# Sparse attention and its filler projections: how many steps run beside each head

## The chip, the cores and the metric

The kernel runs on one core of a Trainium2 chip. The metric is the device time of one execution in microseconds (us). Three executions of the kernel before gave 1282.54, 1283.15 and 1283.22 us; the median is 1283.15 us.

## The reference, cut to what matters

A first block (sequence of 256 tokens, width 1024) projects the normed input once and splits the result. Eight sparse-attention heads in two groups use three branches, a retention branch uses four heads, and two sets of merge gates weigh the branches:

```python
proj = h @ w_in
q_nsa, kv_nsa, g_nsa, q_ret, k_ret, v_ret, g_ret, g_merge = split(proj)
# compressed branch: 15 blocks of keys; softmax over them, per head
p_cmp = masked_softmax(q @ kc.T * scale, mask_cmp);  o_cmp = p_cmp @ vc
# selected and window branches: both see all causal keys at this length
o_slc = masked_softmax(q @ k_slc.T * scale, causal) @ v_slc
o_win = masked_softmax(q @ k_win.T * scale, causal) @ v_win
o = g0 * o_cmp + g1 * o_slc + g2 * o_win
```

The projections that fill TensorE's time beside the heads are `v_ret` (two units of 512 columns, `vr0` and `vr1`), `g_ret` (`sg0`, `sg1`) and the first quarter of `g_merge` (`gm0`, `gm1`, 256 columns each). Retention, a feed-forward block, and then two layers of another network follow; the change doesn't touch them.

## The kernel before

**Weights.** All weights are packed in chunks of at most 128x2048 f32 and come over SP's queue into six `raw` buffers. ScalarE (ACT) rounds a chunk to `whi` (L1102), VectorE (DVE) or GpSimd subtracts to get the rest, `wlo` (L1761 on DVE), and TensorE multiplies three times for each product: high by high, high by low, low by high. In the stage of the change all splits are DVE's. Each engine's program runs strictly in its written order. A split is written `AHEAD` = 3 chunks before the use: whoever takes chunk i in the back queue first splits all up to i + 3. ACT's `whi` must also wait until the chunk four back has been used up.

**The back queue.** `rows` (L545) yields after each two products of three matmuls with 512 columns: a unit of two chunks is eight steps, four for each chunk. `feats` (L566) yields after one k: six matmuls with 256 columns, eight steps for a unit of one chunk. The queue beside the heads is `vr0` (steps 1 to 8), `vr1` (9 to 16), `sg0` (17 to 24), `sg1` (25 to 32), `gm0` (33 to 40) and `gm1` (41 to 48). The first step of each chunk (1, 5, 9, ..., 29, 33, 41) splits the chunk three on; on DVE step 5 splits none and step 9 splits two. A finished half of a unit is copied out of PSUM, the first half by DVE (steps 6, 14, 22, 30), the second half by ACT (8, 16, 24, 32); a finished gate unit by ACT (40, 48).

**The front.** PE, ACT and DVE each have a generator `nsa` (L792, L1299, L2092) that emits its own part of the attention, and `weave` (L205) runs a number of back steps at each yield: two if nothing else is said. There are two blocks of 128 tokens. For each, `compressed` makes the scores of the compressed branch (PE), their softmax (DVE and ACT), the transpose of the probabilities (L747) and the product with the values. Then come eleven places s for the eight heads u: at place s, PE transposes the probabilities of head s-2 (L776), multiplies those of head s-3 with the values, and makes the scores of head s (both L528). DVE at place s copies the transposed probabilities of head s-2 out if s is even (`ET`, L1803), gathers four heads' outputs if s-3 is the fourth (L2075 to L2089, `Tm` first), and takes the maximum of head s (L2059). ACT at place s copies `ET` of head s-2 if s is odd (L1296) and takes the exponentials of head s (L1288). Places run from 0 to 10 for the first block and from 8 to 18 for the second.

**What waits for what.** The transpose of head u waits for its exponentials and for `ET` of head u-1 (one bank holds them). The values of head u wait for `ET` of head u and, for u = 4 or 12, for `Tm` of the head before. The scores of head u wait for the exponentials of head u-2.

With two steps at each yield, PE's queue of 48 steps ends after place 13. Places 14 to 18 have none beside them.

The two loops that decide it:

```python
def weave(front, back, n):
    for m in front:
        steps(back, n if m is None else m)
    run(back)
```

Of the kernel before, what the change touches and what calls it, by code (L numbers as in the profile page):

```python
# [132 lines left out]
class Count:  # L133
# [6 lines left out]
    def at(self, sem, *names, by=1):  # L140

        self.now[sem] += by
        self.name(sem, *names)
        return SEM.get(sem), by
# [7 lines left out]
    def on(self, *name):  # L152

        return ("d_out", 0) if self.known is None else self.known[name]
# [35 lines left out]
def run(g):  # L190
    for _ in g:
        pass
# [7 lines left out]
def steps(g, n):  # L200
    for _ in range(n):
        next(g, None)

def weave(front, back, n):  # L205

    for m in front:
        steps(back, n if m is None else m)
    run(back)

def bc(ap, shape, ax):
# [7 lines left out]
def tok(tt):  # L220
    return slice(tt * 128, tt * 128 + 128)
# [284 lines left out]
def pe_program(pe, t, ev, pb):  # L506
# [20 lines left out]
    def product(o, a, b, start=True, stop=True, names=()):  # L527
        signalled(pe.op.matmul(o, a, b, start=start, stop=stop, skip_group_check=True), names, "pe_small")  # L528
# [148 lines left out]
    def ret_turned(w, tt):  # L677
        turned((w, "T", tt), [(w, "rot", tt)], t.ra[2 * (w == "kr") + tt][:, :], 4)
# [55 lines left out]
    def compressed(tt):  # L734
        for k in range(2):
            pe.wait_ge(*on("free", ("qT", k, 1)))
            pe.wait_ge(*on("free", ("kT", k)))
        pe.wait_ge(*on("kc lo"))
        if tt:
            pe.wait_ge(*on("exp", 6))  # L740
        for j in range(8):
            product(t.sc[0][:, j * 32:j * 32 + 32], t.q1[:, j, tok(tt)], t.kcs[:, :, j % 2, :],
                    names=[("cmp scores", tt)] * (j == 7))
        yield
        pe.wait_ge(*on("cp", tt))
        pe.wait_ge(*on("VC") if tt == 0 else on("ET", 7))
        pe.op.transpose(t.tp[0:120, 0:128], t.cp[:, :], ident).then_inc(*at("pe_turned", ("cpT", tt)))  # L747
        yield
        pe.wait_ge(*on("cpT out", tt))
        if tt:  # L750
            pe.wait_ge(*on("Tm", 7))
        product(t.ob[:, :], t.cpT[:, :], t.VC[:, :, :], names=[("o cmp", tt)])
        yield

    def scores(u):
        tt, hd = units[u]
        gr, b, n = hd // 4, hd % 4, 128 * (tt + 1)
        bk = t.sc[u % 2]
        for k in range(2):
            pe.wait_ge(*on("free", ("kT", k)))  # L760
        pe.wait_ge(*on("cmp masked", tt) if u % 8 < 2 else on("exp", u - 2))
        for k in t.k1h, t.k1l:
            product(bk[:, :].rearrange("p (a k) -> p a k", a=2)[:, :, 0:n], t.q1[:, 2 * b + gr, tok(tt)],
                    k[:, gr, :, 0:n], k is t.k1h, False)
        pe.wait_ge(*on("idb"))
        pe.wait_ge(*on("mkb"))
        for a in range(2):
            product(bk[:, a * S + n - 128:a * S + n], t.idb[:, :], t.mkb[:, :], False, True, [("scores", u)] * a)

    def probs_turned(u):  # L770
        nk = units[u][0] + 1
        pe.wait_ge(*on("exp", u))
        pe.wait_ge(*on("cpT out", units[u][0]) if u % 8 == 0 else on("ET", u - 1))
        for a in range(2):
            for k in range(nk):
                ins = pe.op.transpose(t.tp[:, (a * nk + k) * 128:(a * nk + k) * 128 + 128],  # L776
                                      t.Ex[u % 3][:, a, k * 128:k * 128 + 128], ident)
        ins.then_inc(*at("pe_turned", ("ExT", u)))

    def values(u):  # L780
        tt, hd = units[u]
        gr, nk = hd // 4, tt + 1
        pe.wait_ge(*on("ET", u))
        if u % 4 == 0:
            pe.wait_ge(*on("oa cmp", tt) if u % 8 == 0 else on("Tm", u - 1))
        for a in range(2):
            for k in range(nk):
                product(t.ob[:, ((hd % 4) * 2 + a) * 64:((hd % 4) * 2 + a) * 64 + 64], t.ET[u % 2][:, a * nk + k, :],
                        t.qkv[k][:, 896 + 256 * a + 64 * gr:896 + 256 * a + 64 * gr + 64], k == 0, k == nk - 1,
                        [("pv", u)] * (a == 1 and k == nk - 1))  # L790

    def nsa():  # L792
        yield
        n = 0
        for tt in range(2):
            for _ in compressed(tt):
                yield
                n += 1
                if n == 3:
                    ret_turned("kr", 0)  # L800
            for s in range(8 * tt, 8 * tt + 11):
                if 8 * tt <= s - 2 < 8 * tt + 8:
                    probs_turned(s - 2)
                if 8 * tt <= s - 3:
                    values(s - 3)
                if s < 8 * tt + 8:
                    scores(s)
                yield
                n += 1
                if n == 5:  # L810
                    ret_turned("kr", 1)
# [264 lines left out]
def act_program(act, t, ev, pb):  # L1076
# [222 lines left out]
    def nsa():  # L1299
        yield  # L1300
        n = 0
        for tt in range(2):
            for _ in compressed(tt):
                yield
                n += 1
                if n == 3:
                    ret_turned("kr", 0)
            for s in range(8 * tt, 8 * tt + 11):
                if 8 * tt <= s - 2 < 8 * tt + 8 and s % 2:
                    probs_out(s - 2)  # L1310
                if s < 8 * tt + 8:
                    exps(s)
                yield
                n += 1
                if n == 5:
                    ret_turned("kr", 1)
# [411 lines left out]
def dve_program(dve, t, ev, pb):  # L1728
# [288 lines left out]
    def compressed(tt):  # L2017
        madd, m01 = (small(t, n).rearrange("p (t c) -> p t c", t=2)[:, tt, 0:15] for n in ("madd", "m01"))
        mx, l, r = t.rt[:, 0:8], st[:, 480:488], st[:, 488:496]
        dve.wait_ge(*on("cmp scores", tt))  # L2020
        s = t.sc[0][:, 0:256].rearrange("p (b g a c) -> p g b a c", g=2, a=2, c=16)[:, :, :, :, 0:15]
        cs4 = t.cs[:, :, :].rearrange("p (g b) c -> p g b c", g=2)
        dve.op.tensor_tensor(cs4, s[:, :, :, 0, :], madd.unsqueeze(1).unsqueeze(1).to_broadcast([128, 2, 4, 15]),
                             ALU.add).then_inc(*at("dve_small"))
        await_own()
        dve.op.tensor_tensor(cs4, s[:, :, :, 1, :], cs4, ALU.add).then_inc(*at("dve_small", ("cmp masked", tt)))
        await_own()
        dve.op.tensor_reduce(mx, t.cs[:, :, :], AXX, ALU.max).then_inc(*at("dve_small"))
        await_own()
        dve.op.tensor_tensor(t.cs[:, :, :], t.cs[:, :, :], bc(mx, [128, 8, 15], 2), ALU.subtract).then_inc(  # L2030
            *at("dve_small", ("cs less max", tt)))
        yield None if tt else 0
        dve.wait_ge(*on("cs exp", tt))
        dve.op.tensor_reduce(l, t.cs[:, :, :], AXX, ALU.add).then_inc(*at("dve_small"))
        await_own()
        dve.op.reciprocal(r, l).then_inc(*at("dve_small"))
        await_own()
        dve.wait_ge(*on("gates"))
        dve.op.tensor_tensor(r, r, gates[:, tt, :, 0], ALU.mult).then_inc(*at("dve_small"))
        if tt:  # L2040
            dve.wait_ge(*on("cpT", 0))
        dve.op.tensor_tensor(t.cp[:, :].rearrange("p (h c) -> p h c", h=8), t.cs[:, :, :], bc(m01, [128, 8, 15], 1),
                             ALU.mult).then_inc(*at("dve_small", ("cp", tt)))
        if tt == 0:
            yield 4
        copied([("cpT out", tt)], t.cpT[0:120, :], t.tp[0:120, 0:128], ("cpT", tt))
        yield
        yield
        dve.wait_ge(*on("o cmp", tt))
        await_own()  # L2050
        dve.op.tensor_tensor(t.oa[tt][:, :].rearrange("p (h d) -> p h d", h=8),
                             t.ob[:, :].rearrange("p (h d) -> p h d", h=8), bc(r, [128, 8, 64], 2),
                             ALU.mult).then_inc(*at("dve_out", ("oa cmp", tt)))
# [38 lines left out]
    def nsa():  # L2092
        yield 0
        for tt in range(2):
            yield from compressed(tt)
            for s in range(8 * tt, 8 * tt + 11):
                if 8 * tt <= s - 2 < 8 * tt + 8 and s % 2 == 0:
                    probs_out(s - 2)
                if 8 * tt <= s - 3 and (s - 3) % 4 == 3:
                    values(s - 3)  # L2100
                if s < 8 * tt + 8:
                    score_max(s)
                yield

    qr_read, kr_read = ([(w, "T", tt) for tt in range(2)] for w in ("qr", "kr"))
    back = chain(
# [541 lines left out]
```

## Time and profile before

| | before |
|---|---|
| runs (3) | 1282.54, 1283.15, 1283.22 us; median 1283.15 us |
| profiled execution, its own time | 1283.58 us |
| its span, first to last instruction | 1282.3 us |
| mean granted TensorE clock | 0.999 |
| PE busy | 1270.8 us (99% of the span) |
| DVE busy | 891.4 us (70%) |
| ACT busy | 689.4 us (54%) |
| PE's share of the chain that ended last | 95% |

The profiled execution took 0.4 us more than the median; 1.3 us of its time lie outside the span. A row of the timeline gives start, duration, engine, line, operation, output and inputs, shapes, and in brackets the idle time before it and what ended that. The stage of the change lies between about 84 and 170 us. All times of rows are us from the start of the span. Ends of matmuls are modelled, so the distance between two starts tells more of PE than the durations do.

### The profile page before, as it was taken

How to read it: one execution, taken by the hardware profiler on the slowest of the kernel's cores; microseconds unless marked ns; L12 is line 12 of the kernel's file. 1: busy time of each engine (PE TensorE's matmuls, PEld its weight loads, DVE VectorE, ACT ScalarE, POOL GpSimd, SP SyncE).
4: the chain of work that ended last, by engine and by line, in shares of the span. 5: the costliest groups of instructions: out<-in, count | busy, mean ns of one | idle time of the engine just before them, and what ended most of it. 6: DMA issues, size and time to landing. Idle time of an engine off the chain costs nothing.

```text
span 1282.3 us, 20063 instructions
## 1 busy us (share of the span) xinstructions
PE 1270.8 (99%) x8232; PEld 1152.3 (90%) x8232; DVE 891.4 (70%) x1308; ACT 689.4 (54%) x992; POOL 357.6 (28%) x270
## 2 busy tenths in 40 slices
PE   8999999999999999999999999999999999999999
PEld 7988889989999879899998888888999999888887
DVE  6765665768888468986567777646898476877752
ACT  6655445366655355466746555435456674655541
POOL 0210021014440059476450000007857633000000
PEclk9999999999999999999999999999999999999999
DMA  9654234555555546734464555544854444555551
GB/s 348 235 191 152 110 116 142 187 185 193 177 186 196 192 143 235 235 134 155 141 213 165 197 181 183 194 164 175 280 184 139 158 154 176 189 177 192 196 190 42
DMA packets 36572, 230.83 MB, mean 180 GB/s; under 512 B 4480, under 2 KB 5120, under 8 KB 10496
## 3 DMA queue, kind: packets, MB, share of 16 engines
q1 hardware_dynamic: 36480, 229.55, 50.6%
q8 instruction: 65, 1.06, 0.3%
q14 instruction: 27, 0.22, 0.0%
HBM read 222.19 MB, written 1.05 MB: 174 GB/s over the span
## 4 chain that ended last, share of the span: by engine, by line
PE 95%; DVE 2%; DMA 1%; POOL 1%; ACT 1%; SPq 0%; issue 0%; DVEq 0%; POOLq 0%
PE ps L604 13%; PE ps L582 12%; PE ps L584 12%; PE ps L583 12%; PE ps L523 11%; PE ps L525 11%; PE ps L524 11%; PE ps L607 7%; PE ps L528 5%; PE ps L542 1%; DMA raw<-in_w 1%; PE ps L1014 1%; SPq L428 0%; PE ps L776 0%; POOL sg L1658 0%
## 5 line engine op out<-in xcount | busy, mean ns | idle before, releaser
L1102 ACT ACTIVATE whi<-raw 128x2048 fp32r<-128x2048 f32 x205 | 390.2, 1906 | 164.8 <-PE ps L525 95.7
L1761 DVE TENSOR_TENSOR wlo<-raw,whi 128x2048 fp32r<-128x2048 f32 (+1 forms) x165 | 379.8, 2304 | 135.8 <-ACT whi L1102 134.9
L582 PE MATMUL ps<-hh,whi 128*128 128x256 f32 x992 | 283.6, 286 | 0.0
L584 PE MATMUL ps<-hh,wlo 128*128 128x256 f32 x992 | 280.7, 283 | 0.0
L583 PE MATMUL ps<-hh,whi 128*128 128x256 f32 x992 | 280.6, 283 | 0.0
L1636 POOL TENSOR_TENSOR wlo<-raw,whi 128x512 fp32r<-128x512 f32 x160 | 203.6, 1304 | 135.6 <-ACT whi L1102 132.6
L604 PE MATMUL ps<-hh,whi 128*128 128x512 f32 x704 | 192.6, 395 | 0.0
L583 PEld LDWEIGHTS ps<-hh,whi 128*128 128x128 f32 x992 | 190.1, 192 | 0.4 <-issue 0.2
L582 PEld LDWEIGHTS ps<-hh,whi 128*128 128x128 f32 x992 | 190.1, 192 | 0.4 <-issue 0.2
L584 PEld LDWEIGHTS ps<-hh,wlo 128*128 128x128 f32 x992 | 190.1, 192 | 0.0
L1608 POOL TENSOR_TENSOR st<-st,sm 128x1 f32<-128x1 f32 (+2 forms) x28 | 48.3, 1725 | 403.2 <-DVE st L1814 310.7
L604 PEld LDWEIGHTS ps<-hh,whi 128*128 128x128 f32 x704 | 120.4, 189 | 16.3
L607 PEld LDWEIGHTS ps<-hh,wlo 128*128 128x128 f32 x704 | 108.0, 189 | 15.0
L523 PE MATMUL ps<-whi,hh 128*128 128x512 f32 (+1 forms) x272 | 108.8, 400 | 3.3 <-DVE hh L1873 1.4
L607 PE MATMUL ps<-hh,wlo 128*128 128x256 f32 x704 | 112.0, 281 | 0.0
L525 PE MATMUL ps<-whi,hh 128*128 128x512 f32 (+1 forms) x272 | 105.2, 387 | 0.0
L524 PE MATMUL ps<-wlo,hh 128*128 128x512 f32 (+1 forms) x272 | 105.2, 387 | 0.0
L523 PE MATMUL ps<-whi,ghi 128*128 128x512 f32 x264 | 102.9, 390 | 0.0
L524 PE MATMUL ps<-wlo,ghi 128*128 128x512 f32 x264 | 102.7, 389 | 0.0
L525 PE MATMUL ps<-whi,glo 128*128 128x512 f32 x264 | 102.7, 389 | 0.0
L2362 DVE SCALAR_TENSOR_TENSOR ps<-gp,sm,ps 128x256 f32<-128x256 f32 x232 | 99.3, 483 | 0.0
L1424 ACT ACTIVATE fu<-ps 128x512 f32<-128x512 f32 x44 | 26.3, 598 | 108.4 <-PE ps L607 108.4
(311 smaller groups left out, 2099.3 us busy)
## 6 DMA issues: line engine op xcount, KB each, us to landing
raw<-in_w SPq DMA_DIRECT2D x203, 1024.0 KB, 4.8
raw<-in_w SPq DMA_DIRECT2D x8, 256.0 KB, 6.3
kst<-kh SPq DMA_DIRECT2D x16, 128.0 KB, 2.6
qst<-qh SPq DMA_DIRECT2D x16, 128.0 KB, 2.4
raw<-in_w SPq DMA_DIRECT2D x2, 560.0 KB, 16.8
x<-in_x SPq DMA_DIRECT2D x2, 512.0 KB, 5.1
gain<-in_rows SPq DMA_DIRECT2D x2, 512.0 KB, 10.7
kst<-kl SPq DMA_DIRECT2D x8, 128.0 KB, 2.5
```

Of the source, the lines that this page charges most:

```text
L523: pe.op.matmul(o, sh, mh, start=start, stop=False, skip_group_check=True)
L524: pe.op.matmul(o, sh, ml, start=False, stop=False, skip_group_check=True)
L525: signalled(pe.op.matmul(o, sl, mh, start=False, stop=stop, skip_group_check=True), names)
L582: pe.op.matmul(o, wh[:, k, c:c + 128], hi[:, k, :], start=first, stop=False, skip_group_check=True)
L583: pe.op.matmul(o, wh[:, k, c:c + 128], lo[:, k, :], start=False, stop=False, skip_group_check=True)
L584: ins = pe.op.matmul(o, wl[:, k, c:c + 128], hi[:, k, :], start=False, stop=last, skip_group_check=True)
L604: pe.op.matmul(o[:, :], wh[:, k, c], t.hh[:, k, :, :], start=k == 0, stop=False, skip_group_check=True)
L607: ins = pe.op.matmul(o[:, 0:S], wl[:, k, c], t.hhi[:, k, :], start=False, stop=k == 7, skip_group_check=True)
L1102: act.op.activation(t.whi[i % NHI][:, 0:n], t.raw[i % NRAW][:, 0:n], ACT.Copy).then_inc(*at("act_hi", ("hi", i)))
L1636: pool.op.tensor_tensor(t.wlo[i % NRAW][:, half(k)], t.raw[i % NRAW][:, half(k)], t.whi[i % NHI][:, half(k)].bitcast(F32), ALU.subtract).t ...
L1761: dve.op.tensor_tensor(t.wlo[i % NRAW][:, c], t.raw[i % NRAW][:, c], t.whi[i % NHI][:, c].bitcast(F32), ALU.subtract).then_inc(*at("dve_lo ...
L2362: ins = dve.op.scalar_tensor_tensor(t.cv[:, f, :] if j == 30 else acc, t.gp[:, f, j:j + S], cw[:, f, j:j + 1], acc, ALU.mult, ALU.add)
```

## The change

A new function gives the number of steps beside a place, and the three `nsa` generators yield it after each place. PE's `compressed` yields 2 + tt after the scores, and PE's `nsa` hands on what it yields; ACT's and DVE's `compressed` are as before.

```diff
+def beside(s):
+    return 1 if 3 <= s < 8 else 2

@@ PE, compressed(tt), after the compressed scores
-        yield
+        yield 2 + tt
         pe.wait_ge(*on("cp", tt))
@@ PE, nsa()
-            for _ in compressed(tt):
-                yield
+            for m in compressed(tt):
+                yield m
@@ PE, ACT and DVE, nsa(), after each place s
-                yield
+                yield beside(s)
```

Steps done when a place (or a yield of `compressed`) is over, as the two programs write them:

| | s=2 | 3 | 4 | 5 | 6 | 7 | 8 | 9 | 10 | compressed: 1, 2, 3 | 8 | 9 | 10 | 11 | 12 | 13 | 14 | 15 |
|---|---|---|---|---|---|---|---|---|---|---|---|---|---|---|---|---|---|---|
| before, all three engines | 14 | 16 | 18 | 20 | 22 | 24 | 26 | 28 | 30 | 32, 34, 36 | 38 | 40 | 42 | 44 | 46 | 48 | | |
| after, PE | 14 | 15 | 16 | 17 | 18 | 19 | 21 | 23 | 25 | 28, 30, 32 | 34 | 36 | 38 | 40 | 42 | 44 | 46 | 48 |
| after, ACT and DVE | 14 | 15 | 16 | 17 | 18 | 19 | 21 | 23 | 25 | 27, 29, 31 | 33 | 35 | 37 | 39 | 41 | 43 | 45 | 47 |

## Rows read from the trace of the kernel before

**Rows 1.** The page, part 1: busy time of each engine.
```profile
PE 1270.8 (99%) x8232; PEld 1152.3 (90%) x8232; DVE 891.4 (70%) x1308; ACT 689.4 (54%) x992; POOL 357.6 (28%) x270
```

**Rows 2.** Waits of PE in the whole run, first row: total us, times, longest.
```profile
PE ps L523 <- DVE hh L1873: 1.4, 1, 1.4
```

**Rows 3.** Timeline of PE, place 3 of the first block and place 4's start.
```profile
105.52 0.38 PE L776 MATMUL ps<-sm,Ex 128*128 128x128 f32 x2
...
106.11 0.37 PE L528 MATMUL ps<-k1h,q 128*128 128x256 f32 x1
...
106.53 0.48 PE L523 MATMUL ps<-whi,hh 128*128 128x512 f32 x1
...
109.35 0.38 PE L776 MATMUL ps<-sm,Ex 128*128 128x128 f32 x2
```

**Rows 4.** Timeline of DVE, places 4 to 6 of the first block.
```profile
110.58 0.42 DVE L2059 TENSOR_REDUCE st<-ps 128x2 f32<-128x256 f32 x1 [0.39 <-PE ps L528]
113.75 2.29 DVE L1761 TENSOR_TENSOR wlo<-raw,whi 128x2048 fp32r<-128x2048 f32 x1 [2.75 <-ACT whi L1102]
115.96 0.42 DVE L2059 TENSOR_REDUCE st<-ps 128x2 f32<-128x256 f32 x1
117.45 0.42 DVE L1803 COPY ET<-ps 128x256 f32<-128x256 f32 x1 [1.07 <-PE ps L776]
...
118.22 0.69 DVE L2081 TENSOR_TENSOR Tm<-ps,st 128x512 f32<-128x512 f32 x1
...
119.75 0.42 DVE L2059 TENSOR_REDUCE st<-ps 128x2 f32<-128x256 f32 x1
```

**Rows 5.** Timeline of ACT, place 4 of the first block, later a copy and a `whi`.
```profile
111.04 0.37 ACT L1288 ACTIVATE Ex<-ps,st 128x128 f32<-128x128 f32 x1 [0.39 <-DVE st L2059]
...
111.74 1.91 ACT L1102 ACTIVATE whi<-raw 128x2048 fp32r<-128x2048 f32 x1
...
126.87 0.60 ACT L1135 ACTIVATE sg<-ps 128x512 f32<-128x512 f32 x1
...
131.81 1.92 ACT L1102 ACTIVATE whi<-raw 128x2048 fp32r<-128x2048 f32 x1 [2.27 <-PE ps L525]
```

**Rows 6.** Timeline of PE, from the first block's last values to place 16.
```profile
131.55 0.55 PE L528 MATMUL ps<-qkv,ET 128*128 128x64 f32 x4
...
139.20 0.32 PE L747 MATMUL ps<-sm,cp 128*120 128x128 f32 x1 [0.61 <-DVE cp L2042]
...
143.08 0.40 PE L528 MATMUL ps<-k1h,q 128*128 128x512 f32 x1
...
145.15 0.40 PE L528 MATMUL ps<-k1h,q 128*128 128x512 f32 x1
...
147.23 0.60 PE L776 MATMUL ps<-sm,Ex 128*128 128x128 f32 x4
...
149.75 0.60 PE L776 MATMUL ps<-sm,Ex 128*128 128x128 f32 x4
...
165.57 0.63 PE L776 MATMUL ps<-sm,Ex 128*128 128x128 f32 x4 [1.40 <-ACT ET L1296]
```

**Rows 7.** Timeline of DVE, from the end of the first block to place 9.
```profile
133.83 2.29 DVE L1761 TENSOR_TENSOR wlo<-raw,whi 128x2048 fp32r<-128x2048 f32 x1
...
136.64 0.27 DVE L2023 TENSOR_TENSOR cs<-ps,sm 128x120 f32<-128x120 f32 x1
...
145.95 0.69 DVE L2059 TENSOR_REDUCE st<-ps 128x2 f32<-128x512 f32 x1 [1.34 <-PE ps L528]
```

**Rows 8.** Timeline of ACT, place 10 of the second block.
```profile
149.19 0.47 ACT L1288 ACTIVATE Ex<-ps,st 128x256 f32<-128x256 f32 x1 [1.00 <-DVE st L2059]
...
150.10 1.91 ACT L1102 ACTIVATE whi<-raw 128x2048 fp32r<-128x2048 f32 x1
```

**Rows 9.** Stretches: busy us of PE, PEld, DVE, ACT, POOL; granted clock; DMA share; GB/s.
```profile
10.00:11.00 1.00, 1.00 (x3) 0.72 (x3) 1.00 (x6) 1.00 (x3) 0.00 (x0) 0.50 1.03 260
...
160.00:169.90 9.90, 8.47 (x69) 7.49 (x68) 5.07 (x12) 5.52 (x14) 0.00 (x0) 1.00 0.32 108
```

More of the change, by code:

```diff
@@ L1312, in nsa @@
                     exps(s)
-                yield
+                yield beside(s)
                 n += 1
@@ L2102, in nsa @@
                     score_max(s)
-                yield
+                yield beside(s)
     qr_read, kr_read = ([(w, "T", tt) for tt in range(2)] for w in ("qr", "kr"))
```

## The prediction

> **What bounds the kernel.** I read the page first: PE is busy 99% of the span, DVE 70%, ACT 54% [rows 1]. The change adds and removes no work, so it can only change how long PE waits. The list of PE's waits says how little that is: its first row is a single wait of 1.4 us [rows 2]. The timelines show those in the stage of the change: 0.61 us ahead of the transpose of the second compressed softmax and 1.40 us ahead of place 16's transpose, which is among the places with no steps beside them [rows 6]. Even if both went, the gain is 2.0 us. About 0.2%, 2.6 us, is what a measurement of this kernel can tell from no change. So the question is whether the thinner places 3 to 7 and the shifted weight splits make new waits.
>
> **Prices.** A place of the first block takes 109.35 - 105.52 = 3.83 us: 1.01 us until its first projection matmul and 2.82 us for two row steps, 1.40 each. The scores start 0.59 us into the place [rows 3]. A place with one step takes 2.43. From the scores on, the way through the other engines is: maximum 0.64 us after the scores' start (109.35 + 0.59 = 109.94 to 110.58) [rows 3, 4], exponentials 0.46 later, and 0.70 for them until ACT takes its next instruction [rows 4, 5]. A `whi` on ACT is followed by its `wlo` on DVE 2.01 us after its own start, and DVE's next instruction starts 2.21 after that of the `wlo` [rows 4, 5]. A split that a place emits thus blocks ACT and DVE for 4.2 us in all, and every maximum and `ET` copy behind it in the program waits. Before, the split of step 17 stood at place 4, between the maxima of heads 4 and 5, and nothing was late: head 5's transpose was due at 105.52 + 4 x 3.83 = 120.84, and its `ET` 4 was copied from 117.45 [rows 4].
>
> **Part 1, places 3 to 7.** Up to place 3 nothing differs. Places 4, 5, 6 and 7 then start at 107.95, 110.38, 112.81 and 115.24. Step 17 is now place 5's, behind the maximum and the exponentials of head 5 and ahead of `ET` 4, the gathering of heads 0 to 3 and the maximum of head 6. Scores 5 start at 110.97, maximum 111.61, exponentials 112.07, `whi` 112.77, `wlo` 114.78, `ET` 4 116.99. With 0.42 us for the copy and 0.1 for the signal, the transpose of head 5, due at 115.24, starts at 117.5: a wait of 2.3 us. The values of head 4 come 0.22 us later but need `Tm` 3, which starts 0.77 us after `ET` 4 and lasts 0.69 [rows 4]: to 118.45, a second wait of 0.7. From `ET` 4 to maximum 6 it is 2.3 us (119.75 - 117.45, the gathering of four heads between them) [rows 4], so the exponentials of head 6 are at 119.8 and `ET` 5 stands behind them on ACT; the transpose of head 6 is due at 120.7 and gets its bank at 121.0: 0.25. Together **+3.25 us**. From below 0, if that `wlo` came 3.3 us sooner; from above 3.6, since nothing else is queued there. I take 3.25: each link is a row of the same stage.
>
> **Part 2, the compressed softmax.** In the kernel before, the last values of the block start at 131.55, the `wlo` of step 29 follows the gathering at +2.28, the softmax starts at +5.09 and the transpose at +7.65 [rows 6, 7]. After, place 10 runs steps 24 and 25: the split is step 25's, and its `whi` needs the chunk that step 24 uses up, in the same place, 0.4 (four value matmuls, most of the 0.59 of [rows 3]) + 1.40 after the values' start. Before, the chunk was used up when the values started, and the `whi` followed 0.26 later (131.81) [rows 5, 6]; so 0.26 for the signal, and 0.5 for ACT's copy of `sg0`, which now stands ahead (0.60 long [rows 5]; the next instruction starts about 0.1 before such an end): `whi` at +2.56, `wlo` +4.57. DVE's own copy of `sg1` (0.6) is no longer ahead of the softmax. So the softmax starts at +4.57 + 2.21 = +6.78 and the transpose at 6.78 + (139.20 - 136.64) = +9.34, 1.69 later than before. PE arrives one row step, 1.40, later. The wait thus grows: **+0.3 us**, although PE has three steps there. Bounds: -0.6 (the whole wait goes, if the copy and the split are hidden) and +0.8.
>
> **Part 3, places 8 to 11 of the second block.** Take U for the start of that transpose (before: 139.20). Before, places up to the scores of head 8 took 143.08 - 139.20 = 3.88 with four gate steps at 0.72; after, four row steps: 3.88 + 4 x (1.40 - 0.72) = 6.6. Then places 8, 9 and 10 are 2.07, 2.08 and 2.52 us long [rows 6], with gate steps as before: the transpose of head 9 is due at U + 6.6 + 6.67 = U + 13.27. But step 33, whose split stood well ahead of the heads, is now emitted at place 8, behind maximum 8 and the exponentials of head 8, with ACT's copy of `sg1` also before it. Maximum 8 at U + 6.6 + 0.80 [rows 6, 7] = 7.4; exponentials 0.72 later, 0.91 long [rows 8]: 9.03; the copy 0.5: 9.53; `wlo` +2.01: 11.54; maximum 9 +2.21: 13.75; exponentials 14.47, and 0.9 for them: 15.4. Head 9's transpose waits from 13.27 to 15.45: **+2.2 us**. `ET` 8 is ready at 15.1, just before. Bounds: 0 (if `whi` went ahead of the exponentials, which its place in the program excludes) and 2.5.
>
> **Part 4, the tail.** Step 41's split is at place 12 and 4.2 us long in the same way; but there a full place is about 3.4 us long (2.52 [rows 6] and eight value matmuls), and before it stood at place 10 without a wait. I find the transpose of head 13 due 0.1 us after its exponentials. Places 14 and 15 now have two gate steps each, 1.45 us a place, so the 1.40 us ahead of place 16 are covered but for some 0.3 us in the gathering of four heads; what follows place 16 is as before. **-1.4 us**, between -1.7 and -0.8.
>
> **POOL and SP.** Nothing of POOL's or SP's is moved: raw loads are issued when chunks are used up, six ahead, and no split in this stage waited for one.
>
> **Sum.** 3.25 + 0.3 + 2.2 - 1.4 = +4.35 us. On the profiled execution's 1283.58 that gives 1287.9; the median of the runs is 0.4 lower, so I say **1287.5 us**, 0.34% slower.
>
> **Rival 1: the clock falls as well.** Near the start of the run PE stood idle for 1.4 us, and right after it the granted clock was 0.50, that is 1.2 instead of 2.4 GHz [rows 2, 9]. With the 1.40 us wait in the tail it stayed at 1.00 [rows 9]. The waits of parts 1 and 3 are 2.2 to 3 us of idleness in a stretch of about 3. If it then stays low for three microseconds (assumed; the row shows one), 1.5 us of PE's work are lost: with one of the two +5.9, with both +7.3: 1289 or 1290.5. The rows hold one case of each kind, with the shorter idleness. The Trainium skill ("TensorE: Matmul & The Clock Gate", The HAM clock gate) says that the throttled state is the default and activity releases it; by that rule a long enough hole costs more than itself, which speaks for this rival.
>
> **Rival 2: only one of the two new waits comes.** If ACT or DVE catch up 2 us somewhere, for instance since a split starts sooner than the rows let me place it, the sum is +2.1 (part 1 alone) or +1.1 (part 3 alone): 1284.2 to 1285.3, within 0.2%.
>
> **Rival 3: not slower.** The places decide: if the `wlo` of step 17 began by 112.5 instead of 114.8 and that of step 33 by U + 9.3 instead of U + 11.5, neither transpose would wait, and part 4 alone would count, with part 2: -1.1, 1282.0 us. For it speaks that ACT is busy for only 54% of the run [rows 1]; against it, that the idle time is before instructions which wait for DVE and PE in turn, and the split stands behind these. The Trainium skill ("TensorE: Matmul & The Clock Gate", the table at its head) says ScalarE's and VectorE's queues are strictly first in, first out; that is what the rows show, where maximum 5 starts the moment `wlo` lets DVE go (115.96, 2.21 after the `wlo`) [rows 4] though its scores were made 1.5 us sooner. A gain of more than 0.2% needs every wait of the stage to go, and there are only 2.0 us of them.
>
> **How the numbers follow.** Forecast (both waits, clock kept) 0.50; rival 1 0.20; rival 2 0.15, two thirds of it within 0.2%; rival 3 0.11; something faster that I don't see 0.04. Slower by over 0.2%: 0.50 + 0.20 + 0.05 = 0.75, less 0.02 for the low end of my own forecast. The likeliest case alone is 1286.3 to 1288.5. The range goes down into rival 2 and up through rival 1: 1284.0 to 1290.5.
>
> **What would show it.** After: no wait of 1.4 us for `ET` on ACT at place 16; in its place a wait of about 2.3 us of PE L776 for DVE's `ET` (L1803) and one of L528 for `Tm` in the first block near 117 us; about 2.2 us of L776 for ACT's exponentials (L1288) some 13 us behind the compressed transpose; that transpose's own wait at 0.6 to 1.1. Place 16's transpose (165.57 before) should be at about 169.9, and every later stage as long as before. It would be wrong if `wlo` of step 17 is not between maximum 5 and `ET` 4 on DVE, if the transposes of heads 5 and 9 start without a wait, or if later stages change length.

## The result, and the profile after

| | before | after |
|---|---|---|
| median | 1283.15 us | 1288.38 us |
| runs (5 each) | 1282.54 to 1283.53 | 1286.56 to 1289.38 |
| profiled execution, its own time | 1283.58 us | 1289.06 us |
| its span | 1282.3 us | 1287.8 us |

The medians are 5.23 us apart, 0.41%; the ratio on record, which isn't the quotient of the medians, is 1.0036, with an interval of 1.0023 to 1.0049, or 4.6 us. All rows below give times from the start of the span. The lines of after are six higher than before's (L776 is L782, L528 is L534, L1803 is L1809, L1761 is L1767, L2059 is L2065, L2081 is L2087, L1288 is L1294).

The page's engine totals of after say that the work is the same as before [rows 1]:

```profile
PE 1271.3 (99%) x8232; PEld 1152.4 (89%) x8232; DVE 891.1 (69%) x1308; ACT 689.5 (54%) x992; POOL 357.7 (28%) x270
```

PE's waits in the whole run, after (engine, line, what it waited for: total us, times, longest). Before, the longest was 1.4 us [rows 2]; now two of 2.1 head the list, and the 1.4 us for `ET` on ACT is gone:

```profile
PE ps L782 <- ACT Ex L1294: 2.1, 1, 2.1
PE ps L782 <- DVE ET L1809: 2.1, 1, 2.1
...
PE ps L753 <- DVE cp L2048: 0.9, 1, 0.9
...
PE ps L534 <- DVE Tm L2087: 0.5, 1, 0.5
```

The timeline of PE, after, from place 3 of the first block to place 16 of the second:

```profile
105.08 0.38 PE L782 MATMUL ps<-sm,Ex 128*128 128x128 f32 x2
...
117.20 0.41 PE L782 MATMUL ps<-sm,Ex 128*128 128x128 f32 x2 [2.05 <-DVE ET L1809]
...
118.14 1.01 PE L534 MATMUL ps<-qkv,ET 128*128 128x64 f32 x4 [0.53 <-DVE Tm L2087]
...
122.09 0.38 PE L782 MATMUL ps<-sm,Ex 128*128 128x128 f32 x2
...
128.96 0.55 PE L534 MATMUL ps<-qkv,ET 128*128 128x64 f32 x4
...
138.26 0.33 PE L753 MATMUL ps<-sm,cp 128*120 128x128 f32 x1 [0.91 <-DVE cp L2048]
...
153.73 0.66 PE L782 MATMUL ps<-sm,Ex 128*128 128x128 f32 x4 [2.11 <-ACT Ex L1294]
...
171.21 0.63 PE L782 MATMUL ps<-sm,Ex 128*128 128x128 f32 x4
```

These are the transposes of head 5 (117.20), head 6 (122.09), the second compressed softmax (138.26), head 9 (153.73) and place 16 (171.21), the last now with nothing in brackets. What DVE does ahead of the first wait, after:

```profile
111.26 0.42 DVE L2065 TENSOR_REDUCE st<-ps 128x2 f32<-128x256 f32 x1 [1.71 <-PE ps L534]
114.43 2.29 DVE L1767 TENSOR_TENSOR wlo<-raw,whi 128x2048 fp32r<-128x2048 f32 x1 [2.75 <-ACT whi L1108]
116.64 0.42 DVE L1809 COPY ET<-ps 128x256 f32<-128x256 f32 x1
...
117.40 0.69 DVE L2087 TENSOR_TENSOR Tm<-ps,st 128x512 f32<-128x512 f32 x1
```

Maximum of head 5, then `wlo`, then `ET` 4. Before, the `wlo` stood between the maxima of heads 4 and 5, with as long an idle time before it, and cost nothing [rows 4]. Two things differ: what is queued behind it, and that PE comes back for the `ET` sooner, since the places are thin. Both are needed, by an estimate from the prediction's own prices [rows 3, 4, 5]: with full places and the split behind maximum 5, `ET` 4 would be copied at about 119.8 and ready some 0.5 us before head 5's transpose is due (120.84), and only `Tm` would be about 0.2 late. No run tried that. Stretches of the two holes, after (us, busy us of PE, PEld, DVE, ACT, POOL, granted clock, DMA share, GB/s):

```profile
116.00:119.00 3.00, 1.27 (x7) 1.06 (x7) 2.86 (x8) 0.00 (x0) 0.00 (x0) 0.88 0.00 0
119.00:122.00 3.00, 3.00 (x11) 2.47 (x11) 0.77 (x3) 1.85 (x9) 0.00 (x0) 0.55 0.00 0
122.00:126.00 4.00, 4.00 (x25) 3.34 (x23) 0.42 (x1) 1.60 (x1) 0.00 (x0) 1.00 0.15 25
151.00:154.00 3.00, 0.89 (x8) 0.69 (x7) 2.82 (x4) 1.17 (x5) 0.00 (x0) 1.00 0.00 0
154.00:157.00 3.00, 3.00 (x27) 2.73 (x26) 0.69 (x1) 1.72 (x6) 0.00 (x0) 1.00 0.02 5
```

Behind the first hole the granted clock is 0.55, which is nearly all 1.2 GHz; behind the second, where PE did even less, it stays at 1.00. So this execution shows the forecast and, once, the clock of rival 1. (In stretches of 1 us the clock is below 1.00 from 118 to 122 and nowhere else in this run; the profiled execution of before has its only such stretches at 9 to 14, near the start of the run.)

**The stage's length** is a measure that leaves the rest of the run out: from place 3's transpose to the first scores of the retention that follows the second block. Before it is 63.81 us (105.52 to 169.33), after 69.88 (105.08 to 174.96): 6.07 longer, while the span is 5.5 longer and the stage begins 0.44 sooner.

### The profile page after: what moved, and what is told of

Its sections match the earlier page's. It is cut to its first block, busy times and chain, and to the rows that moved or that the text cites. A ratio compares the mean times of both kernels' runs of the same rounds, so it can differ in the third digit from the quotient of the medians.

```text
span 1287.8 us, 20063 instructions
## 1 busy us (share of the span) xinstructions
PE 1271.3 (99%) x8232; PEld 1152.4 (89%) x8232; DVE 891.1 (69%) x1308; ACT 689.5 (54%) x992; POOL 357.7 (28%) x270
## 4 chain that ended last, share of the span: by engine, by line
PE 95%; DVE 2%; ACT 2%; DMA 1%; POOL 1%; issue 0%; SPq 0%; DVEq 0%; POOLq 0%
PE ps L610 13%; PE ps L588 12%; PE ps L590 12%; PE ps L589 12%; PE ps L529 11%; PE ps L531 11%; PE ps L530 11%; PE ps L613 6%; PE ps L534 5%; PE ps L548 2%; PE ps L1020 1%; DVE wlo L1767 1%; DMA raw<-in_w 0%; ACT whi L1108 0%; PE ps L782 0%; POOL sg L1664 0%
## 5 line engine op out<-in xcount | busy, mean ns | idle before, releaser
L1767 DVE TENSOR_TENSOR wlo<-raw,whi 128x2048 fp32r<-128x2048 f32 (+1 forms) x165 | 379.6, 2304 | 140.0 <-ACT whi L1108 139.3
```

The lines of the kernel that those rows point to most:

```text
L1767: dve.op.tensor_tensor(t.wlo[i % NRAW][:, c], t.raw[i % NRAW][:, c], t.whi[i % NHI][:, c].bitcast(F32), ALU.subtract).then_inc(*at("dve_lo ...
```

## The experiments

The theory (T): each new wait is made by DVE's `wlo`, which stands in the program ahead of an `ET` or a maximum that PE will soon need, and holds DVE until ACT's `whi` is done. The ten kernels e1 to e10 are described one by one below. Rivals: the order of PE against the other engines makes the waits (P); the granted clock makes most of the time (C); thinner places are harmful by themselves, since each leaves less of PE's work above a head's way through the other engines (B). Ratios are to the kernel before on the same chip, as they are on record; they aren't the quotients of the medians, and differ from them by up to 0.0008 (e5). Before took 1283.3, 1283.8 and 1282.6 us in the three batches (29, 26 and 23 runs).

| kernel | median us (runs) | ratio, interval | stage us |
|---|---|---|---|
| e1 | 1291.16 (6) | 1.0057, 1.0039 to 1.0074 | 71.74 |
| e2 | 1281.88 (12) | 0.9987, 0.9974 to 1.0000 | 64.66 |
| e3 | 1280.34 (12) | 0.9976, 0.9966 to 0.9986 | 61.39 |
| e4 | 1283.59 (12) | 1.0002, 0.9990 to 1.0015 | 64.67 |
| e5 | 1285.55 (12) | 1.0006, 0.9994 to 1.0019 | 65.24 |
| e6 | 1287.64 (12) | 1.0029, 1.0018 to 1.0039 | 67.55 |
| e7 | 1289.05 (9) | 1.0035, 1.0023 to 1.0048 | 71.49 |
| e8 | 1297.61 (6) | 1.0102, 1.0087 to 1.0117 | 77.63 |
| e9 | 1288.84 (12) | 1.0046, 1.0030 to 1.0063 | 69.60 |
| e10 | 1287.27 (12) | 1.0029, 1.0018 to 1.0039 | 68.40 |

One caution for all of them. The kernel before itself takes 1282 to 1288 us on these chips, and its time goes with its mean granted clock: in the three batches the executions at 0.998 or more have medians of 1282.4, 1282.9 and 1282.5 us, those at 0.997 or less 1286.0, 1286.5 and 1287.5. Medians of kernels that drew different shares of the two can't be set beside each other to within 2 us. The waits of the profiled executions can. The stage's length can once the clock's part in it is told, for it is of one execution only, and not always a typical one: e5's and e6's were the fastest of their twelve (1283.85 and 1285.44 us) and held the clock longer than most, e2's (1284.70) was among the slowest. And not all of this scatter is of the stage: in the profiled executions of before, e1, e3, e4 and e8 the clock also fell between 9 and 18 us, where all kernels are alike, in e3 for about 7 us and only there.

### One part of the change at a time: e1, e2

e1 leaves out the extra steps of PE's compressed softmax:

```diff
@@ PE, compressed(tt)
-        yield 2 + tt
+        yield 2
```

> The changed kernel with PE's compressed branch back at two steps; the thin places 3 to 7 stay, so PE, ACT and DVE now do the same number of steps everywhere. Theory (new waits come from where the weight splits of steps 17, 25 and 33 stand among the heads): the waits for ET 4 and Tm 3 near head 5 stay as in the changed kernel (about 2.1 and 0.5 us); PE reaches the compressed transpose one row step (1.4 us) sooner while DVE's chain is as late, so that wait grows from 0.9 to about 2.5 us; the wait of head 9's transpose shrinks by 0.7 to about 1.5 us, since one more row step is done before it; a gate step more is left for the tail. In all 0 to +0.7 us against the changed kernel, 1288 to 1289. Rival (PE running one step ahead of ACT and DVE is what makes the waits): head 9's wait goes and the time falls to about 1286.

e2 keeps those and makes every place full again:

```diff
 def beside(s):
-    return 1 if 3 <= s < 8 else 2
+    return 2
```

> The kernel before with only PE's extra step after the second compressed scores; two steps at every place. Theory: no split moves, so no new wait; the 0.6 us ahead of the compressed transpose is covered by the gate step (0.7), place 13 has one step less and its successors come sooner, the 1.4 us wait at place 16 stays. 1282.2 to 1283.1, -0.7 to 0 us. Rival (PE ahead of ACT and DVE costs): over +1 us, with a wait of a transpose for exponentials near head 9.

Timeline of PE, e1, the compressed transpose and head 9's:

```profile
140.43 0.32 PE L753 MATMUL ps<-sm,cp 128*120 128x128 f32 x1 [2.27 <-DVE cp L2048]
...
155.89 0.66 PE L782 MATMUL ps<-sm,Ex 128*128 128x128 f32 x4 [1.43 <-ACT Ex L1294]
```

The wait for `cp` is 1.36 longer than in after, one row step. That prices the extra step: PE's third step covers 1.4 us of the softmax, and the thinner places are what made the softmax late. Head 5's transpose waits 2.1 us with or without that step (118.11), so the order of PE (P) makes none of the first hole. Nor does it make the second: head 9's wait is 1.43 without that step, where P wanted it gone. e1's time is 2 us above its expectation, and its stage 1.86 longer than after's. Some 1.3 of this is behind head 5, where the stretches show the clock low for two whole stretches, not one, and 0.6 is the gate step left for the tail (place 16's transpose to the end of the stage: 4.36 us against 3.75).

```profile
119.00:122.00 3.00, 2.95 (x11) 2.66 (x12) 1.61 (x4) 1.65 (x8) 0.00 (x0) 0.50 0.00 0
```

The next, 122 to 125, is at 0.50 too. In e2 the compressed wait is gone and the one in the tail stays. In its profile the clock fell behind that 1.40 us wait, which it had not in before's. The row is from e2's timeline of PE:

```profile
164.14 0.63 PE L782 MATMUL ps<-sm,Ex 128*128 128x128 f32 x4 [1.40 <-ACT ET L1302]
```

and this from e2's stretches:

```profile
166.00:169.00 3.00, 3.00 (x17) 3.00 (x16) 0.00 (x0) 2.40 (x2) 0.00 (x0) 0.51 0.04 8
```

The stage is 64.66 long for that reason: 63.81 less the 0.61 of the compressed wait, and 1.5 of clock. e2's ratio is 0.13% below 1, with 1 at the edge of its interval; its median is 0.3 us below what was expected.

### The places kept, the low parts moved: e3 and e4

e3 is the changed kernel, e4 the kernel before, each with one edit on DVE: a split asked for in a back step is emitted three steps later. (While `held_back` holds a list, `splits` only notes down what it was asked for.)

```diff
@@ DVE
+    held_back = [None]
+
     def splits(last):
 
+        if held_back[0] is not None:
+            held_back[0].append(last)
+            return
...
+    def later(g, n, only):
+        due, step = [], 0
+        while True:
+            step += 1
+            held_back[0] = []
+            over = next(g, "over") == "over"
+            asked, held_back[0] = held_back[0], None
+            for last in asked:
+                due.append((step + (n if not only or step in only else 0), last))
+            while due and (due[0][0] <= step or over):
+                splits(due.pop(0)[1])
...
-    weave(nsa(), back, 2)
+    weave(nsa(), later(back, 3, ()), 2)
```

> The changed kernel, but DVE emits each low-part split of this queue three steps later than ACT emits its whi; no step of PE or ACT moves. Theory (the split blocks DVE between a maximum and the ET copy while ACT's whi is still running): wlo of step 17 then stands at place 8, that of step 33 at place 10, both with their whi long done. The waits before heads 5 and 9 go, that before the compressed transpose goes (chain at +7.1 against PE's arrival at +8.2 after the last values), and only some 0.2 us of the tail wait is left: 1281 to 1282, -1 to -2 us against before and -7 against the changed kernel. Rival (a place with one step is too short for the chain scores, maximum, exponentials, ET whatever is split where): the waits before heads 5 to 7 stay, over 1286.

> The kernel before with the same lateness of DVE's low-part splits (three steps). Theory: before, the full places hide the splits anyway, so lateness alone gains nothing: the compressed chain keeps one wlo inside it (0.6 us wait stays), the 1.4 us of place 16 come from the gathering of four heads and stay. 1282.7 to 1283.5, within 0.5 us of before. Rival (late low parts are a gain by themselves, so that the third run's result says nothing about the moved steps): 1 us or more below before.

Timeline of DVE, e3 (its lines are five higher again: L1814 is `ET`, L2070 the maximum, L1772 `wlo`):

```profile
114.29 0.42 DVE L1814 COPY ET<-ps 128x256 f32<-128x256 f32 x1 [1.18 <-PE ps L782]
...
119.24 0.42 DVE L1814 COPY ET<-ps 128x256 f32<-128x256 f32 x1 [1.22 <-PE ps L782]
119.58 2.28 DVE L1772 TENSOR_TENSOR wlo<-raw,whi 128x2048 fp32r<-128x2048 f32 x1
```

`ET` 4 is copied at 114.29 instead of 116.64, though this stage began 1.38 us later (106.46), DVE waits for PE and no longer the other way, and the `wlo` has no idle time before it: `whi` was long done. PE's waits in the whole run of e3 hold no L782 and no L753:

```profile
PE ps L529 <- DVE hh L1884: 2.0, 1, 2.0
PE ps L548 <- DVE xn L1833: 1.2, 1, 1.2
PE ps L649 <- POOL zero L1626: 1.0, 1, 1.0
PE ps L534 <- DVE STt L2168: 0.8, 1, 0.8
```

The stage is 61.39 us, 8.5 less than after's and 2.4 less than before's. At 1280.34 us e3 beats both kernels, 0.24% below before and 0.7 us below the expected range. Of the 3.0 us by medians some 0.8 go with the clock: 10 of e3's 12 executions are at 0.998 or more, 20 of before's 29, and among those alone it is 1280.26 against 1282.45, 2.2 us, near the stage's 2.4. Places 3 to 7 are as thin in e3 as in the changed kernel, so B falls in their case: the thinning costs nothing once no `wlo` that must wait for its `whi` stands in the way. And e4 shows that lateness alone brings nothing: with the steps where they were, the tail's wait of 1.40 stays and the compressed one grows from 0.61 to 1.48, more than expected. Waits of PE, e4:

```profile
PE ps L747 <- DVE cp L2047: 1.5, 1, 1.5
PE ps L776 <- ACT ET L1296: 1.4, 1, 1.4
```

### One split at a time: e5 and e6

Both are the changed kernel with the same wrapper, in e5 for step 17's split alone, in e6 for step 33's:

```diff
-    weave(nsa(), back, 2)
+    weave(nsa(), later(back, 3, (17,)), 2)
```

> The changed kernel with DVE's wlo of step 17 alone emitted three steps later (at place 8 instead of place 5). Theory: the waits for ET 4 and Tm 3 go, with what follows them (3.25 us and, where the clock fell there, about 1.5 more); the compressed wait (0.9), head 9's (2.1) stay. 1283.7 to 1285.3. Rival (thin places are too short by themselves): the wait before head 5 stays, 1288.

> The changed kernel with DVE's wlo of step 33 alone emitted three steps later (place 10 instead of place 8). Theory: head 9's wait of 2.1 us goes, all else stays: 1286.0 to 1286.6, 2.1 us below the changed kernel. Rival (head 9 waits because its place comes too soon after the scores, not for the split): no change, or a wait of the same length for the exponentials.

First row of PE's waits in e5, and then in e6, where each took away one of after's two:

```profile
PE ps L782 <- ACT Ex L1294: 2.1, 1, 2.1
```

```profile
PE ps L782 <- DVE ET L1814: 2.1, 1, 2.1
```

In e5 the wait for `Tm` went too, and the clock stayed up: the stage fell by 4.64 (2.05 + 0.53, the clock's 1.5 and 0.5 more). In e6, where the clock fell behind the first hole as in after, it fell by 2.33, against a wait of 2.11. So each hole belongs to one split, as T says. By its ratio e5 is 0.06% above before (by the medians 0.14%), and its 1285.55 us are a little over what I expected. In e6 the median fell only from 1288.38 to 1287.64 where 2.1 us were expected; 11 of its 12 executions had a mean clock of 0.997 or less, and by the time alone e6 is inconclusive.

### Is it the split, or the places? e8 and e9

If T holds, other thin places must make a hole elsewhere: where the split of step 21 then falls.

```diff
-    return 1 if 3 <= s < 8 else 2
+    return 1 if 5 <= s < 10 else 2
```

> The changed kernel with the thin places at 5 to 9 instead of 3 to 7. Theory (the wait follows the split): step 17's split is back at place 4 and hurts nobody; step 21's now stands at place 7, ahead of ET 6, so heads 5 and 6 pass without a wait and the transpose of head 7 waits about 2.8 us for ET 6 on DVE; the compressed wait and head 9's stay. 1287 to 1288.5. Rival (it is head 5, with the gathering of heads 0 to 3 behind it, that can't stand a thin place): places 5 and 6 are still thin, so the wait stays at heads 5 and 6.

This edit reaches further than it should have: places 8 and 9 of the second block are thin as well, which no theory's numbers had counted. The whole time (1297.61 us, where 1287 to 1288.5 were expected; three waits of `ET`, the longest 3.5) thus tests nothing, though the first block already has its one wait at head 7 (125.34, 2.65). e9 limits it to the first block, with `1 if tt == 0 and 5 <= s < 10 else 2`:

> As the run with thin places 5 to 9, but in the first block only; that run thinned places 8 and 9 of the second block as well, which I had overlooked, and three waits for ET came of it. Steps from place 10 on are now those of the changed kernel. Theory (the wait follows the split): no wait before heads 5 and 6, 2.7 us before head 7's transpose for ET 6 (as that run's trace showed), 0.9 before the compressed transpose, 2.1 before head 9's. The sum of the waits is that of the changed kernel less 0.2, so 1286.5 to 1289. Rival (thin places late in the block are worse in themselves): 1291 or more, with further waits.

Timeline of DVE and then of PE, e9:

```profile
112.67 2.29 DVE L1767 TENSOR_TENSOR wlo<-raw,whi 128x2048 fp32r<-128x2048 f32 x1 [2.75 <-ACT whi L1108]
114.87 0.42 DVE L2065 TENSOR_REDUCE st<-ps 128x2 f32<-128x256 f32 x1
...
118.28 0.42 DVE L2065 TENSOR_REDUCE st<-ps 128x2 f32<-128x256 f32 x1 [0.37 <-PE ps L534]
121.63 2.29 DVE L1767 TENSOR_TENSOR wlo<-raw,whi 128x2048 fp32r<-128x2048 f32 x1 [2.92 <-ACT whi L1108]
123.84 0.42 DVE L1809 COPY ET<-ps 128x256 f32<-128x256 f32 x1
```

```profile
112.10 0.38 PE L782 MATMUL ps<-sm,Ex 128*128 128x128 f32 x2
...
114.58 0.38 PE L782 MATMUL ps<-sm,Ex 128*128 128x128 f32 x2
...
117.05 0.38 PE L782 MATMUL ps<-sm,Ex 128*128 128x128 f32 x2
...
119.53 0.38 PE L782 MATMUL ps<-sm,Ex 128*128 128x128 f32 x2
...
124.40 0.41 PE L782 MATMUL ps<-sm,Ex 128*128 128x128 f32 x2 [2.65 <-DVE ET L1809]
```

The transposes of heads 3 to 6 start 2.47 us apart with nothing in brackets, and that of head 7 waits 2.65: the hole moved by two places with the split behind maximum 7. Before it stand three thin places in a row without a wait. The three rows "maximum, `wlo`, `ET`" are in the same order as in after. And the `wlo` of step 17 (112.67), back ahead of maximum 5, costs nothing although thin places follow. Its 1288.84 us are within the expected range.

### The clock: e7 and e10

e7 adds, ahead of head 5's transpose, 16 matmuls on operands that are ready, into a bank whose contents are not used; they change no result and keep PE at work during the hole. e10 adds as many ahead of head 9's.

```diff
@@ PE, nsa()
             for s in range(8 * tt, 8 * tt + 11):
+                if s in (7, 11):
+                    pe.wait_ge(*(on("exp", 5) if s == 7 else on("oa cmp", 1)))
+                    for _ in range(16):
+                        product((t.sc[1] if s == 7 else t.ob)[:, 0:256], t.q1[:, 0, tok(0)], t.k1h[:, 0, 0, :])
```

(e7 has `if s == 7` and the first of each pair.)

> The changed kernel with 16 matmuls of 256 columns (some 1.9 us) added on PE ahead of head 5's transpose, where it waits 2.05 us; they write a bank that the scores of head 7 then overwrite, and change no result. Theory (the granted clock fell after that hole, and matmuls at 0.43 instead of 0.23 us cost 1.3 to 1.5 us): the transpose starts as late as before, the clock stays at 1.00 between 116 and 122 us, and the time falls by about 1.3 us to 1286.5 to 1287.3, with less scatter. Rival (the clock's fall is hidden by the next wait, and the scatter has another cause): 1288 to 1289 as the changed kernel.

> The changed kernel with the 16 filler matmuls ahead of head 5's transpose and 16 more ahead of head 9's, into a bank that head 8's values then overwrite. Theory (each hole can let the granted clock fall, and one filled hole left the fall to the other): the clock is 1.00 through the whole stage, every mean clock is 0.998 or above, the transposes start as late as before, and the median is 1286.3 to 1287.5, below both the changed kernel (1288.4) and the run with one filled hole (1289.1). Rival (the scatter has other causes than the holes): median still 1288 to 1289 with mean clocks of 0.997 and below.

Stretches of e7. Behind the first hole, now filled, the clock is 1.00; behind the second, where after's profile had 1.00, it fell:

```profile
119.00:122.00 3.00, 3.00 (x18) 2.36 (x18) 1.12 (x4) 1.78 (x9) 0.00 (x0) 1.00 0.00 0
150.00:153.00 3.00, 0.89 (x6) 0.74 (x5) 2.35 (x4) 1.64 (x7) 0.00 (x0) 0.86 0.00 0
153.00:156.00 3.00, 3.00 (x15) 2.48 (x13) 0.00 (x0) 1.00 (x3) 0.00 (x0) 0.50 0.00 0
```

The stage is 71.49 us long, 1.6 more than after's, since the clock was low for some 7 us here. So the time of e7 is no better than after's, and my expectation of a gain was a miss: the hole of head 9 can take the clock down too. It needn't, for in e5's profile, where it is the only hole as here, the clock stayed up. In e10 both are filled. Its stretches:

```profile
116.00:119.00 3.00, 2.35 (x17) 1.82 (x16) 2.86 (x9) 0.12 (x1) 0.00 (x0) 1.00 0.00 0
119.00:122.00 3.00, 3.00 (x18) 2.31 (x17) 0.61 (x2) 1.65 (x9) 0.00 (x0) 1.00 0.00 0
...
150.00:153.00 3.00, 2.81 (x26) 2.61 (x24) 1.83 (x4) 2.15 (x9) 0.00 (x0) 1.00 0.00 0
```

The median is as expected; 10 of its 12 executions have a mean clock of 0.998 or more, where all were expected to. The matmuls fill the holes but leave the cause, so what remains over before is the late transposes alone: 4.6 us by the stage (68.40 - 63.81), and 4.6 by the medians of the executions at 0.998 or more (1287.16 against 1282.53). C is thus the smaller part: 1.5 us between the two profiled stages (69.88 - 68.40). By the ratios (1.0036 of after, 1.0029 of e10) it would be 0.9 us of the whole, but their intervals overlap, and the whole times don't show it.

## Why the prediction came out right

It said 1287.5 us, and the median is 1288.38, within the range; the sum was +4.35, and +5.2 came by the medians, +4.6 by the ratio. In e10, where the clock holds, the stage is 4.59 longer than before's: that is what the sum was worked out for. Step by step:

- **Part 1** (+3.25). The `wlo` of step 17 is between maximum 5 and `ET` 4. Head 5's transpose starts 12.12 us after place 3's, where 11.98 was worked out; the waits are 2.05 and 0.53, where 2.3 and 0.7 stood. The third wait, 0.25 at head 6, isn't there: the low clock behind the hole made PE later than its bank. In e7, with the clock up, head 6's transpose comes 2.46 us after the values before it, where a thin place has 2.26, so some 0.2 of it is. The whole part is 3.16 there: 15.53 us from place 3's transpose to head 6's, against 12.37 in e5. e5 shows that the split of step 17 makes both waits.
- **Part 2** (+0.3). From the last values to the compressed transpose 9.30 us, worked out 9.34; the wait went from 0.61 to 0.91. In e1 the `cp` wait is one row step longer, as the sum had it.
- **Part 3** (+2.2). The transpose of head 9 starts 15.47 us after the compressed one, worked out 15.45, and waits 2.11. e6 shows that it is step 33's.
- **Part 4** (-1.4). Place 16's transpose waits for nothing. It starts at 171.21, where I had about 169.9, and 66.13 us after place 3's instead of 64.4: 1.5 of this is the low clock ahead of it, and the rest is an error in this term. The prediction left some 0.3 us of the gathering of four heads uncovered and yet took off all of the 1.40; by its own words the term is -1.1, and the sum +4.65. The rows say -1.2: 17.48 us between the transposes of head 9 and place 16, against 15.82 before, with four more gate steps of 0.72 in between. The 0.3 is at place 15, which takes 3.74 in after and 3.42 in e3.
- **Rival 1.** What the sum lacked. I gave the low clock 0.20 as a case of its own and left it out of the sum; in fact it belongs to the forecast, in part of the executions. In after's profile it cost 1.48 us (17.01 from place 3's transpose to head 6's, and 15.53 in e7, where the clock stayed up), close to the 1.5 assumed; in e1 it lasted longer, in e7 it came at the other hole, in e5 and e9 it spared the hole of head 9. A mean of one fall in about two executions would give the 0.85 us that the medians have over the sum; that is arithmetic that fits, not something that the runs count. That the sum came this near is in part luck: part 4 was 0.2 to 0.3 too good, and how often the clock falls was not known.
- **Rival 2** falls: both waits came. **Rival 3** named the right point: e3 is that case, since there the `wlo` no longer stands between a maximum and an `ET`. It gave -1.1 us for this; e3 gained 3.0 on before by medians and 2.4 in the stage, since with it the compressed wait went too (all 2.0 us of waits in the stage), and the stage is 0.4 shorter still.

Of the clock, the Trainium skill ("TensorE: Matmul & The Clock Gate", The HAM clock gate) was cited for the half rate being the default that activity releases. The rows bear out only a part of it: where the holes are filled (e10) the stretches stay at 1.00, and where they are not some fall to 0.50; but the first microsecond of the runs of before and after has 1.00 with PE hardly at work (0.01 us before), so no run here shows the half rate as the default. No run here shows by what rule one hole of 2.1 us takes the clock down and the next does not.

**Left open:** what decides in which execution the clock falls, since the same kernel shows both; and so what exactly the medians of e5 and e6 are worth. Whether a split ahead of an `ET` would cost anything with full places was only estimated. That the low parts' lateness of three steps is the best one wasn't tried.

## What to carry to other kernels

When work is moved between places of a hand-woven program, price each instruction that it issues by what stands behind it on its own in-order engine, and by how soon the bottleneck engine needs that. Here the same `wlo`, with the same 2.75 us of idle time before it, cost nothing ahead of maximum 5 (before and in e9) and 2.6 us of waits ahead of `ET` 4; the `wlo` of step 33 cost 2.1 ahead of maximum 9, because head 9's transpose followed close behind. Where one engine's instruction waits for a long one of another engine (ACT's `whi`, then DVE's `wlo`), emit the second some steps later than the first, and only then thin or thicken the places; neither edit was worth anything without the other, and together they gave 0.24% (e3; 2.4 us of the stage). Compare stages and waits, not only medians, where the clock differs between executions.

## What the runs showed of the hardware

- Behind a single wait of 1.4 us, which ended at 164.14, TensorE's granted clock went to 0.51 and 0.50 for two stretches of 3 us (e2, 166 to 172), while behind the same wait in before's profile [rows 9] and one of 2.1 us in after's it stayed at 1.00. That the wait made it fall is inferred: in the stage the clock fell only behind such waits, in none of the two profiles without one (e3, e10).
- By stretches of 1 us, the low clock of the stage lasted some 3 us in after, e6 and e9, and some 7 in e1, e2 and e7, though PE was at work for all or nearly all of that time.
- The clock also falls where the change has no part: between 9 and 18 us in the profiles of before, e1, e3, e4 and e8, behind waits of 1.4 to 2.9 us, and not in those of after (1.8), e5 (1.9) and e10 (1.4).
- Executions whose mean clock is 0.997 or less took 3.6 to 5 us longer than those at 0.998 or more in before (1286.0 to 1287.5 against 1282.4 to 1282.9) and 4.3 in e9 (1292.0 against 1287.7), but only 1.2 in e3 and e10 and 0.4 in e5.
- The wait for `hh` near the start of the run, which every kernel has and no edit touches, was 1.3 us in e6 and 2.9 in e1: scatter in one single row can be a third of what the change costs.
